# A hybrid encoder layer on eight cores: LN1 of the second token half moved into the first FFN pass

## The reference

```
merged = gates[0] * y_conv + gates[1] * y_attn + gates[2] * y_mem
x = layer_norm(2**0.25 * x + merged @ w_o, ln1_g, ln1_b)
gate, up = split(x @ w_ffn_in, 2)          # 2 x 2816 columns
ffn = (silu(gate) * up) @ w_ffn_out
return layer_norm(2**0.25 * x + ffn, ln2_g, ln2_b)
```

## Time and profile before

| | |
|---|---|
| median of 3 runs (lowest, highest) | 1043.11 us (1041.96, 1046.8) |
| the profiled execution | 1045.4 us, span 1044.4 us on core 0, the slowest of 1035.1 to 1044.4 us |
| busy: PE, DVE, ACT, POOL | 965.2, 557.8, 415.5, 306.0 us (92%, 53%, 40%, 29% of the span) |
| waits of PE for other engines and DMAs, five longest kinds | 16.4, 15.7, 8.8, 7.1, 4.7 us |
| mean granted clock of PE, core 0 | 0.980 |

### The profile page before, as it was taken

How to read it: one execution, slowest core, us unless ns; L and a number is a source line. 1 busy time by engine, 2 the same in 40 slices (tenths; PEclk the granted TensorE clock), 3 DMA queues, 4 the chain that set the end, 5 groups by cost and what they waited for, 6 DMA issues and landing times.

```text
span 1044.4 us, 16309 instructions; the slowest of 8 cores (1035.1 to 1044.4 us)
## 1 busy us (share of the span) xinstructions
PE 965.2 (92%) x5509; PEld 449.9 (43%) x5606; DVE 557.8 (53%) x939; ACT 415.5 (40%) x616; POOL 306.0 (29%) x292
## 2 busy tenths in 40 slices
PE   4999999987999999999998588999999599999996
PEld 1455544543443444444444144444444244444442
DVE  1324566665652222223399766666565466674554
ACT  1135565756552222222256354544222244443211
POOL 3200000211233343323255322355442133333331
PEclk9999999998999999999999899999999899999999
DMA  8994044744469999330362223378533322220222
GB/s 130 192 174 104 11 92 105 100 93 62 62 90 139 141 121 179 49 122 0 112 232 102 100 95 107 102 163 168 155 135 107 124 94 85 81 91 11 81 101 81
DMA packets 39393, 112.12 MB, mean 107 GB/s; under 512 B 4944, under 2 KB 16856, under 8 KB 38192
## 3 DMA queue, kind: packets, MB, share of 16 engines
q0 software_dynamic: 11104, 41.16, 27.1%
q1 hardware_dynamic: 28208, 69.91, 21.1%
HBM read 132.49 MB, written 30.47 MB: 156 GB/s over the span
## 4 chain that ended last, share of the span: by engine, by line
PE 76%; DVE 9%; DMA 7%; issue 4%; ACT 1%; SPq 1%; POOL 1%; DVEq 0%; ACTq 0%; POOLq 0%
PE ps L233 76%; DMA arena<-xt 2%; DMA arena<-w_bf_cache 2%; DVE mvt L1028 2%; DMA arena<-w_out 2%; DVE arena L1063 1%; SPq L147 1%; DMA arena<-u_scratch 1%; DVE arena L1036 1%; DVE arena L1040 1%; DVE arena L1162 1%; DVE mvt L1025 1%; DVE arena L806 1%; POOL arena L147 0%; ACT arena L645 0%
## 5 line engine op out<-in xcount | busy, mean ns | idle before, releaser
L233 PE MATMUL ps<-arena 128*128 128x512 bf16 (+5 forms) x5099 | 947.0, 362 | 68.7 <-DMA arena<-xt 16.4
L233 PEld LDWEIGHTS ps<-arena 128*128 128x128 bf16 (+2 forms) x5196 | 429.2, 98 | 570.9 <-issue 124.5
L837 DVE SCALAR_TENSOR_TENSOR arena<-arena,ps 128x512 f32<-128x512 f32 x96 | 65.8, 686 | 147.0 <-PE ps L233 143.0
L1169 POOL TENSOR_TENSOR arena<-arena 128x512 bf16<-128x512 f32 x66 | 87.8, 1330 | 180.5 <-DVE arena L1162 171.3
L816 ACT ACTIVATE arena<-ps,bgate_sb 128x512 f32<-128x512 f32 x96 | 65.8, 687 | 166.6 <-PE ps L233 166.6
L1159 ACT COPY arena<-ps 128x512 f32<-128x512 f32 x132 | 77.0, 586 | 138.2 <-PE ps L233 134.5
L1162 DVE TENSOR_TENSOR arena<-arena,ps 128x512 f32<-128x512 f32 x132 | 88.3, 684 | 56.8 <-PE ps L233 56.8
L1045 POOL TENSOR_TENSOR arena<-arena 128x1024 f32<-128x1024 f32 (+1 forms) x28 | 70.1, 2507 | 48.6 <-ACT arena L1044 48.6
L844 POOL TENSOR_TENSOR arena<-arena 128x512 f32<-128x512 f32 x32 | 40.7, 1273 | 125.6 <-DVE arena L837 125.6
L1018 ACT ACTIVATE arena<-arena 128x1024 bf16<-128x1024 f32 x32 | 33.7, 1053 | 101.6 <-DVE arena L1273 91.1
L147 POOL DMA_DIRECT2D arena<-w_g x21 | 11.3, 546 | 171.3 <-PE ps L233 170.2
(11 more groups left out here) (98 smaller groups left out, 474.6 us busy)
## 6 DMA issues: line engine op xcount, KB each, us to landing
arena<-w_bf_cache SPq DMA_DIRECT2D x44, 512.0 KB, 4.1
arena<-u_scratch SPq DMA_DIRECT2D x64, 135.0 KB, 3.8
arena<-x SPq DMA_DIRECT2D x16, 512.0 KB, 9.7
y_scratch<-arena SPq DMA_DIRECT2D x16, 512.0 KB, 2.7
arena<-y_scratch SPq DMA_DIRECT2D x16, 512.0 KB, 3.4
out<-arena SPq DMA_DIRECT2D x16, 512.0 KB, 2.6
arena<-w_f POOLq DMA_DIRECT2D x22, 256.0 KB, 7.0
arena<-w_g POOLq DMA_DIRECT2D x9, 512.0 KB, 12.7
```

The costliest lines, as they stand in the source:

```text
L233: return pe.run(lambda: nc.tensor.matmul(out, lhsT, rhs, start=start, stop=stop, skip_group_check=onto), deps, inc)
L837: t_y = dve.run(lambda: nc.vector.scalar_tensor_tensor(out=gb[r], in0=gb[r], scalar=1.0, in1=ps[:, bk, :], op0=ALU.add, op1=ALU.mult), [tk ...
L1169: return pool.run(lambda: nc.gpsimd.tensor_tensor(out=dst, in0=up, in1=gate, op=ALU.mult), deps)
```

## The change

The blocks of tokens 8 to 15 no longer go through their LN1 in the loop over `d_mm`: the loop runs the chain for blocks 0 to 7 at `tb` 1 to 12, nothing at `tb` 13, and the first two steps for blocks 8 and 9 at `tb` 14 and 15; the eight full steps and two short ones that are left follow the even units 0 to 18 of the first FFN pass. The mean and variance are made by three 128x1 instructions of ACT and one of POOL (`d_small`) in place of three on DVE. `d_C` is always DVE's. The DMA that stores `d_Y` is issued at the start of the next step (`y_pend`). `e_sums(0)` stands at `tb` 13. `f1_period` can be begun in part: the first products of unit 0 stand ahead of and within `d_mm(15)`, those of unit 22 within `f2_block(7)`, with 24 and 8 of its 44 products left. Weights of four units are in SBUF before the first pass, three of them folded in the merge stage; those of units 24 and 25 are loaded at the end of the first pass and folded in `f2_block` 1 and 2. `hb_prep(8)` (ACT and POOL, the first block of LN2's second half) moves behind unit 32, `w2` is loaded from unit 8 on in place of unit 11, four buffers move, and the silu table is loaded before LN1.

```diff
-    w1_free = [[dp2_done], [dp2_done, gb_free[0]], [], []]
+    w1_free = [[dp2_done], [dp2_done, gb_free[0]], [dp2_done, gb_free[1]], []]
...
-    for tb in range(4, 16):
-        load_x(tb, [c_done])
+    for tb in (3, *range(4, 16)):
+        load_x(tb, [c_done, g_done])
+    load_w1(3)
+    t_silu = act.run(lambda: nc.scalar.activation(dnt[:, 0, 0:1], eps_t[:, 0:1], AF.Silu), [c_done, t_eps])
...
+    def d_small(tb):
+        mv = mvt[:, tb % 4, :]
+        sm = hsum[:, 0, tb:tb + 1]
+        d_state["mean", tb] = act.run(lambda: nc.scalar.activation(mv[:, 0:1], sm, AF.Identity, scale=1.0 / D))
+        t1 = act.run(lambda: nc.scalar.activation(mv[:, 1:2], sm, AF.Square, scale=1.0 / D))
+        t2 = act.run(lambda: nc.scalar.activation(
+            mv[:, 3:4], stt[:, tb % 4, 1:2], AF.Identity, bias=eps_t[:, 1:2], scale=1.0 / D), [d_state["st", tb]])
+        t3 = pool.run(lambda: nc.gpsimd.tensor_tensor(out=mv[:, 1:2], in0=mv[:, 3:4], in1=mv[:, 1:2], op=ALU.subtract), [t1, t2])
+        d_state["rs", tb] = ln_rstd(t3, tb, rs16[:, tb:tb + 1])
...
+    def d_chain(t, lo, hi):
+        while y_pend:
+            y_pend.pop(0)()
+        if lo <= t - 4 < hi:
+            d_Tpe(t - 4)
+        if lo <= t < hi:
+            d_S(t)
+            d_small(t)
+        if lo <= t - 4 < hi:
+            d_Tev(t - 4)
+        if lo <= t - 2 < hi:
+            d_C(t - 2)
+        if lo <= t - 1 < hi:
+            d_Y(t - 1)
...
     for tb in range(16):
-        d_mm(tb)
         if tb == 15:
+            tg0 = [t_silu, c_done, g_done, [x1_free[i] for i in range(4)]]
             e_start()
+            f1_begin(0)
+            d_mm(15, lambda: f1_begin(0, True))
+        else:
+            d_mm(tb)
+        if tb == 13:
             e_sums(0, [c_done] + [x1_free[i] for i in range(4)])
         d_H(tb)
-        if tb >= 1 and tb != 8:
-            d_chain(False)
+        if 1 <= tb <= 12:
+            d_chain(tb - 1, 0, 8)
+        elif tb > 13:
+            d_chain(tb - 6, 8, 16)
     for u in range(22):
         f1_period(u, u - 1 if u else None)
-        if u % 2 and chain["k"] < 18:
-            d_chain(True)
-        if u >= 11:
+        if u % 2 == 0 and u < 20:
+            d_chain(10 + u // 2, 8, 16)
+        if u >= 8:
...
-            if tb % 8 < 7:
+            if tb not in (7, 15):
                 hb_prep(tb + 1)
-            f2_block(tb)
+            f2_block(tb, {24: lambda: f1_begin(22), 8: lambda: f1_begin(22, True)} if tb == 7 else {})
+            if tb in (1, 2):
+                fold_w1(23 + tb)
         if P == 0:
-            hb_prep(8)
             for u in range(22, 44):
                 f1_period(u, u - 1 if u > 22 else None)
+                if u == 32:
+                    hb_prep(8)
```

More of the change, by code:

```diff
@@ L945, in _build @@
     ln2t = [V(0, [128, D], F32), V(12, [128, D], F32)]
-    X1 = [V(156.5 + 4 * i, [128, D], F32) for i in range(4)] + [V(68 + 4 * i, [128, D], F32) for i in range(12)]
+    X1 = [V(o, [128, D], F32) for o in (156.5, 160.5, 164.5, 172.5)] + [V(68 + 4 * i, [128, D], F32) for i in range(12)]
     HB = [V(o, [128, D], F32) for o in (112, 58, 62)]
@@ L958, in _build @@
     a_done = pe.tok()
-    gb[0] = V(172.5, [128, 512], F32)
-    gb_free[0] = [gb_free[0], a_done]
+    for i in range(2):
+        gb[i] = V(168.5 + 2 * i, [128, 512], F32)
+        gb_free[i] = [gb_free[i], a_done]
     cache_w1(4)
@@ L980, in load_w2 @@
         w2_tok[j] = load(w2[j], w_f2_d[:, j, :], x1_free[4 + j // 2])
-    w1_free = [[dp2_done], [dp2_done, gb_free[0]], [], []]
+    w1_free = [[dp2_done], [dp2_done, gb_free[0]], [dp2_done, gb_free[1]], []]
     w1_slot = [new_slot("w1") for _ in range(4)]
     def load_w1(u):
-        if u < 44:
+        if u < 44 and u not in w1_tok:
             w1_tok[u] = dma(sp, w1s[u % 4][:, 0:4], w1b_d[u % 22], w1_slot[u % 4], [w1_free[u % 4], w1_raw[u % 22]])
     def fold_w1(u):
-        if u < 44:
+        if u < 44 and u not in w1_folded:
+            w1_folded.add(u)
             w1_tok[u] = fold(w1s[u % 4], w1_tok[u])
+    w1_folded = set()
     t_x, x1_st, x1_free = {}, {}, {}
@@ L1057, in d_mm @@
                         if (half == 0 and kc == 0) else (), inc=(half == 1 and kc == 7))
+            if half == 0:
+                mid()
         d_state["mm", tb] = (bO, tk)
@@ L1170, in times, with f1_period @@
         return dve.run(lambda: nc.vector.tensor_tensor(out=dst, in0=up, in1=gate, op=ALU.mult), deps)
-    def f1_period(cur, prev, fill=lambda: None):
+    def f1_period(cur, prev, fill=lambda: None, part=None):
+        new = cur is not None and cur not in unit
         if cur is not None:
@@ L1190, in f1_period @@
         fill()
-        if cur is not None:
+        if new:
             y, dy = banks.alloc(1)
@@ L1207, in f1_period @@
             fill()
-        if cur is not None:
+        if part == "head":
+            return
+        if cur is not None and "tu" not in unit[cur]:
+            s = unit[cur]
             t = prod(s["x"], W, 6, SA[:, 1], False, [s["t1"], sa_tok[P][2]])
@@ L1236, in f1_period @@
                 t_free["u",]["12"] = t_free["g", iq % 2]["12"] = a_tok[2 * iq + 1, 0]
-        if cur is not None:
+        if cur is not None and part is None:
             fold_w1(cur + 2)
@@ L1288, in hb_prep, with f1_begin @@
         if tb < 16:
[L1289 to L1307, removed]
+            hb_x[tb] = ln_scale_ap(HB[tb % 3], rs16[:, tb:tb + 1], ln1t[:, 1, :], [hb_tok[tb], d_state["rs", tb]])
+    def d_chain(t, lo, hi):
[12 more added lines that the diff above has]
+            d_Y(t - 1)
+    def f1_begin(u, second=False):
+        f1_period(u, None, part="second" if second else "head")
     for tb in range(16):
-        d_mm(tb)
         if tb == 15:
+            tg0 = [t_silu, c_done, g_done, [x1_free[i] for i in range(4)]]
             e_start()
+            f1_begin(0)
[3 more added lines that the diff above has]
+        if tb == 13:
             e_sums(0, [c_done] + [x1_free[i] for i in range(4)])
         d_H(tb)
-        if tb >= 1 and tb != 8:
-            d_chain(False)
-    tg0 = [z_free, c_done, g_done, [x1_free[tb] for tb in range(4)]]
+        if 1 <= tb <= 12:
+            d_chain(tb - 1, 0, 8)
+        elif tb > 13:
+            d_chain(tb - 6, 8, 16)
     w2_order = list(range(22))
@@ L1336, in _build @@
     f1_drain(21, 0)
-    assert chain["k"] == 18 and not w2_order
+    assert not w2_order
+    load_w1(24)
+    load_w1(25)
     f1_done = [e_state["mm"]]
```

64 lines of the change are left out of this document (27 added, 37 removed).

## The result

| | before | after |
|---|---|---|
| median (lowest, highest) | 1044.46 us (1041.96, 1046.8), 4 runs | 1019.19 us (1017.17, 1019.52), 4 runs |
| ratio, 95% interval | | 0.9754 [0.9726, 0.9783] |
| the profiled execution | 1045.4 us | 1019.5 us, span 1018.3 us (core 7), cores 1006.7 to 1018.3 us |
| mean granted clock of the slowest core | 0.980 | 0.989 |

The account below looks back on a forecast made before the run. PE, busy 92%, was bound by waits mainly for DVE, itself held by POOL in LN1. Terms 4.7 + 8.8 + 4.1 - 1.9 + 8.3 + 2.0 - 0.8 - 0.5 = 24.7 us gave median 1018.4, range 1009 to 1031.

Parts of the forecast that it names:

- LN1, 4.7 us: LN1 stage: with POOL's large addition gone, DVE blocks take 3.63 us against PE's 4.0; PE's waits of 4.7 us go.
- The 8.8 of `e_sums`: End of LN1: sums placed earlier are ready before PE wants them, so its 8.8 us wait goes whole.
- The slow clock behind it, 4.1: After the wait for `e_sums`: 32 matmuls would take 7.1 us instead of 9.28 + 1.86, winning 4.1.
- First FFN pass, waits of 10.6: Chain steps behind units 0 to 12 make PE wait 10.6 us in sum, against 8.7 before: 1.9 lost.
- taken as hidden: Units 8 to 12: `w2` and stores share DMA time at no cost, since the fold comes 6 us after the issue.
- rival 3: `w2`, stores and `w1` together make weights late; each late fold in units 8 to 12 adds 1 to 2 us: 1024; chance 0.07.
- The fold of unit 2 ahead, put at nothing: Third fold, 1.66 us, in the merge stage where DVE idles: taken at nothing, at most 1.7 once if uncovered.
- Second pass: wait 2.4: Start of second FFN pass: PE waits 2.4 us where it waited 10.7, without fold or DMA between: 8.3 won.
- The clock was put at even odds (0.8): Second pass: the clock may fall after the 2.4 us wait, costing 1.7; at even odds 0.8 lost.
- `hb_prep(8)` behind unit 32: Second FFN pass: the moved step adds a POOL addition beside a fold, costing 0.5 us (0 to 1.1).
- Small ACT instructions: LN1 blocks: three 128x1 instructions on ACT at 0.21 each, 0.6 us a block, taken at no cost.
- Rival 2: POOL's small steps hold DVE's scaling and centring, two of 0.55 us per chain step: 1030; chance 0.12.

Follow-up runs that it names:

- e2: Kernel after with LN1's scaling of blocks 0 to 7 on ACT and POOL again, small steps as after; ratio to before 0.9732.
- e3: Kernel after with the small steps for mean and variance back on DVE (`ln_tiny`), the rest as after; ratio to before 0.9909.
- e12: Kernel before with only the four sums moved one block earlier, behind the matmuls of block 14; ratio to before 0.9994.
- e1: Kernel after with the sums and the begin of unit 0 back behind block 15; ratio to before 0.9746.
- e13: Kernel before with the scaling of the last three LN1 steps by DVE alone, sums where they were; ratio to before 0.9969.
- e4: Kernel after with the chain steps behind odd units 1 to 19 in place of even units 0 to 18; ratio to before 0.9652.
- e5: Kernel after with the second FFN weights `w2` loaded from unit 11 on instead of unit 8; ratio to before 0.9749.
- e7: Kernel after with the FFN weights of units 24 and 25 neither loaded nor folded ahead; ratio to before 0.9775.
- e6: Kernel after with unit 22 not begun inside block 7, its weights still loaded ahead; ratio to before 0.9756.
- e8: Kernel after with `d_Y` of the first FFN pass behind odd units, the chain still behind even ones; ratio to before 0.9675.
- e9: Kernel after with block 7's LN2 put behind unit 23's second product instead of ahead of the second pass; ratio to before 0.9756.

## Why the prediction was right

**LN1, 4.7 us: right.** Blocks of 3.90, no wait of PE. e2 and e3 split its cause: POOL's large addition holds DVE, as the earlier trace rows were read, but alone it costs nothing (e2), and the small steps alone cost 1.2 (e3). Both together stood in the kernel before.

**The 8.8 of `e_sums`: right in size, its cause only half as told.** The prediction won it by the new place of the sums. e12 makes that move alone in the kernel before and gains nothing; e1 undoes it in the kernel after and loses nothing. The 8.8 were DVE's backlog at the end of LN1, with 2.1 of hold by POOL in the sums (e13). What e1 shows in place of the backlog is an idle DVE: with the chain of blocks 8 to 15 moved out, it waits for PE in blocks 11 to 14. The cheaper chain step isn't needed for that, since neither e2 nor e3, which each put back a half of it, brings a wait for the sums. Whether the cheaper step alone, with the blocks left in place, would have done it no run shows. The working on record took all of it together, so its timeline came out right.

**The slow clock behind it, 4.1: gone.** A second stretch of slow clock isn't the change's: in the window from 522 to 530 us the kernel before ran at a granted clock of 0.81 on its slowest core, first row below, after at 1.00, second row, 8 x 0.19 = 1.5 us.

```profile
522.00:530.00 8.00, 7.91 (x31) 3.35 (x31) 6.64 (x13) 3.52 (x6) 3.46 (x3) 0.81 0.98 335
522.00:530.00 8.00, 8.00 (x45) 3.85 (x43) 7.99 (x9) 3.80 (x11) 3.02 (x6) 1.00 0.98 317
```

Cores 4 to 7 of the kernel before are at 1.00 there. And cores 4 to 7 of e1 and e4, whose work up to this window is that of after, are at 0.83 to 0.88 in the window from 516 to 524. What makes it stays open.

**First FFN pass, waits of 10.6: 12.1 on the slowest core, 11.15 on core 1.** By terms: unit 0 1.36 (1.2), unit 2 1.90 (1.9), units 4 and 6 1.45 (1.5), as worked out, the held fold with them. The error is the place of the text where `w2` and the stores in units 8 to 12 are "taken as hidden": unit 10 had 2.40, and 1.7 of slow clock behind it on that core, as two others had at unit 12. This is rival 3 in part, priced in time by e5 at under its interval. The fold of unit 2 ahead, put at nothing, was also a real part of the gain: the earlier trace rows's wait of 3.43 lay behind a fold that waited for its weights in the kernel before.

**Second pass: wait 2.4, exact.** The fold of unit 24 is 1.7 of the 8.3 (e7). In e6 and in e7 alike the load of its weights goes out ahead of block 7's store and isn't waited for, in e6 without the early begin, in e7 by it; and POOL's hold of the scaling (3.19 for 1.28) is gone in both. How the rest of the 8.3 divides between these no run shows. The clock was put at even odds (0.8), and so it came: behind this 2.40 the next 280 matmuls took 62.28 us on four cores and 60.59 on the other four. The slowest core was one of the first four and lost 1.7.

**`hb_prep(8)` behind unit 32: 1.45, where 0.5 was taken and 1.1 was the bound.** It is the tenth wait, it stands on all eight cores and in every run with this order, and the kernel before has none in this pass. Two instructions of one fold are held, line 807 by a product and line 808 by the addition (0.42 each otherwise). DVE, then POOL, then PE:

```profile
863.17 1.30 DVE L807 TENSOR_TENSOR arena<-arena 128x512 bf16<-128x512 bf16 x1
864.58 2.38 DVE L808 TENSOR_TENSOR arena<-arena 128x512 bf16<-128x512 bf16 x1
```

```profile
864.16 2.52 POOL L1050 TENSOR_TENSOR arena<-arena 128x1024 f32<-128x1024 f32 x1
```

```profile
868.30 1.89 PE L233 MATMUL ps<-arena 128*128 128x512 bf16 x8 [1.45 <-DVE arena L1166]
```

**Small ACT instructions: 0.19, 0.19 and 0.30 us, overlapping**, where 0.6 a block was taken:

```profile
527.92 0.19 ACT L1082 ACTIVATE mvt<-hsum 128x1 f32<-128x1 f32 x1
528.01 0.18 ACT L1083 ACTIVATE mvt<-hsum 128x1 f32<-128x1 f32 x1
528.11 0.30 ACT L1084 ACTIVATE mvt<-stt,eps_t 128x1 f32<-128x1 f32 x1
```

**Rival 2 was wrong about who is held.** DVE's scalings and centrings of LN1 stay at 1.28 to 1.31 in the kernel after (five scalings of LN2 take 3.2, as some did in the kernel before, see the earlier trace rows); POOL's small steps are the longer ones beside them (0.37 and 0.74 in unit 2; at unit 10 the power takes 1.09 beside the fold at 642.51 shown above). POOL:

```profile
642.21 0.19 POOL L1086 TENSOR_TENSOR mvt<-mvt 128x1 f32<-128x1 f32 x1
642.53 1.09 POOL L1037 TENSOR_TENSOR rs<-mvt,eps_t 128x1 f32<-128x1 f32 x1
```

The rule of the Trainium skill ("SBUF — State Buffer", Who interferes with whom) agrees with the large operations (e2: 3.10 for 1.28) and with a fold beside a product; for the small ones no run here shows DVE paying.

**The ledger.** Gone: 4.7 + 8.8 + 4.1 in LN1 and at the sums; 10.7 - 2.4 = 8.3 at the second pass with 2.0 - 1.7 = 0.3 of clock. Come: 12.1 - 8.7 = 3.4 and 1.7 in the first pass, 1.45 by `hb_prep(8)`. Sum 19.7, where the same terms were forecast at 24.7. Four losses were priced too low: the waits of the first pass by 1.5, its clock by 1.7, the clock of the second pass by 0.9 and `hb_prep(8)` by 0.95. The two spans differ by 26.1. 4.0 of these lie ahead of the first transposition of LN1 (532.60 before, 528.58 after), where no term of the forecast is: 0.7 up to the merge stage, and 3.3 of slow clock behind it on core 0 of before, the 1.7 of the earlier trace rows and the stretch above. 2.4 I can't place. So the gains were right place by place, the four errors have one sign, and that the total still fits within 1 us is luck.

## What to carry to other kernels

A wait stands where the late engine is asked, not where it fell behind: before moving the awaited instruction, look whether its engine is idle ahead of it (e12: no; e1: yes). With in-order engines, give each of several equal periods the same load rather than every other one a double one (e8: 8 us), or put the heavier load where no instruction is held by another engine (e4: one line, 10 us). Where two parts of a change guard against the same wait, taking them out one at a time shows neither's worth (e6, e7). When a step is moved, its store and loads move in the DMA queue too; e9 lost there what it won on DVE.

## Unexpected of the hardware

How long PE must stand still for its clock to fall is not one number. In the first pass 32 matmuls take 7.07 us at full speed. Behind no wait of 1.90 us or less did they take 8.75. Behind 1.98 (e6, e9), 1.99 (e2, e5), 2.27 (cores 0 and 5 of after), 2.31 (e3) and 2.40 (core 7) they did, but behind 1.98 (e2), 1.99, 2.20 and 2.21 (cores 5, 2 and 0 of after), one 2.31 of e3 and even 2.76 (its cores 0 and 4) they took 7.07. The 2.40 at the second pass brought the granted clock to 0.50 on four cores of after, and left it at 1.00 on core 3 of e8. So among these waits of 2 us and more equal ones can differ by 1.7 us; what decides between them stays open.
